# The last feed-forward block's second projection and last norm: from channels on the partitions to tokens on the partitions

## The reference

```python
def layer_norm_2(x, g, b):
    xf = x.astype(F32)
    mu = jnp.mean(xf, -1, keepdims=True)
    var = jnp.mean(jnp.square(xf - mu), -1, keepdims=True)
    return ((xf - mu) * lax.rsqrt(var + LN_EPS) * g.astype(F32) + b.astype(F32)).astype(x.dtype)

def swiglu(x, w13, w2):
    g, u = jnp.split(x @ w13, 2, axis=-1)
    return (jax.nn.silu(g) * u) @ w2

def second_block(x, ...):
    h = x
    for i in range(DEPTH_2):          # DEPTH_2 = 2
        ...                           # the mixer of the layer
        h = layer_norm_2(DEEPNORM_ALPHA * h + mix, ln1_g[i], ln1_b[i])
        h = layer_norm_2(DEEPNORM_ALPHA * h + swiglu(h, f_w13[i], f_w2[i]), ln2_g[i], ln2_b[i])
    return h
```

## Time and profile before

| | |
|---|---|
| median of 3 runs | 1181.61 us (1177.98 to 1183.34) |
| the profiled execution | 1179.46 us, of which 1177.7 us are the span of the core |
| PE busy | 1121.2 us (95%), 8872 matmuls |
| DVE busy | 811.3 us (69%) |
| ACT busy | 620.0 us (53%) |
| granted PE clock, mean | 0.986 of full speed |
| DMA | 194.7 MB, mean 165 GB/s; weight loads 359 of 512 KB |

### The profile page before, as it was taken

One profiled execution on the slowest core, in us unless ns is written; L12 is line 12 of the kernel. 1 busy time (PEld: TensorE's weight loads), 2 busy tenths in 40 slices (PEclk: granted clock), 3 DMA queues, 4 the chain that ended last, 5 costly groups with the idle time before them and its releaser, 6 DMA issues.

```text
span 1177.7 us, 21218 instructions
## 1 busy us (share of the span) xinstructions
PE 1121.2 (95%) x8872; PEld 1090.4 (93%) x8872; DVE 811.3 (69%) x1363; ACT 620.0 (53%) x1035; POOL 3.3 (0%) x13
## 2 busy tenths in 40 slices
PE   7999989999999998889989999999999999999998
PEld 7998878899999997679989999999999899999997
DVE  7987489878877786586766755555688657555554
ACT  5567444556465558733444645454455546454542
POOL 0000000000000000000000000000000000000000
PEclk9999999999999998989989999999999999999999
DMA  9984247256766613233223365556345335556500
GB/s 371 410 335 167 73 143 286 90 196 222 246 209 203 207 63 108 62 104 122 91 72 126 114 207 184 194 183 195 108 162 193 116 104 161 192 185 190 186 1 36
DMA packets 58128, 194.71 MB, mean 165 GB/s; under 512 B 10801, under 2 KB 11185, under 8 KB 57905
## 3 DMA queue, kind: packets, MB, share of 16 engines
q1 hardware_dynamic: 58032, 193.35, 48.8%
HBM read 192.02 MB, written 1.31 MB: 164 GB/s over the span
## 4 chain that ended last, share of the span: by engine, by line
PE 72%; DVE 17%; ACT 7%; issue 2%; DMA 1%; SPq 1%; ACTq 0%; DVEq 0%
PE ps L500 60%; DVE lo L1434 4%; PE ps L679 3%; ACT hi L970 2%; PE ps L507 2%; DVE raw L1421 2%; PE ps L598 2%; DVE B L1443 1%; PE ps L519 1%; DVE st L1451 1%; DVE ev L1672 1%; DVE B L1456 1%; DVE ev L1669 1%; DVE B L1747 1%; PE ps L685 1%
## 5 line engine op out<-in xcount | busy, mean ns | idle before, releaser
L500 PE MATMUL ps<-hh,hi 128*128 128x256 f32 x1792 | 510.5, 285 | 14.9 <-DVE hl L1468 3.5
L500 PE MATMUL ps<-hl,hi 128*128 128x256 f32 x1792 | 503.6, 281 | 0.0
L500 PE MATMUL ps<-hh,lo 128*128 128x256 f32 x1792 | 503.4, 281 | 0.0
L1434 DVE TENSOR_TENSOR lo<-raw,hi 128x1024 fp32r<-128x1024 f32 x311 | 378.2, 1223 | 172.4 <-ACT hi L970 171.6
L500 PEld LDWEIGHTS ps<-hh,hi 128*128 128x128 f32 x1792 | 340.7, 190 | 18.9 <-issue 9.3
L970 ACT ACTIVATE hi<-raw 128x1024 fp32r<-128x1024 f32 x311 | 324.6, 1052 | 54.7 <-PE ps L500 52.2
L500 PEld LDWEIGHTS ps<-hl,hi 128*128 128x128 f32 x1792 | 340.8, 190 | 0.3
L500 PEld LDWEIGHTS ps<-hh,lo 128*128 128x128 f32 x1792 | 340.6, 190 | 0.0
L500 PE MATMUL ps<-fh,hi 128*128 128x256 f32 x568 | 160.1, 282 | 3.3 <-ACT B L1074 2.5
L500 PE MATMUL ps<-fl,hi 128*128 128x256 f32 x568 | 159.0, 280 | 0.0
L500 PE MATMUL ps<-fh,lo 128*128 128x256 f32 x568 | 158.9, 280 | 0.0
(11 more groups left out here) (242 smaller groups left out, 1084.2 us busy)
## 6 DMA issues: line engine op xcount, KB each, us to landing
raw<-in_w SPq DMA_DIRECT2D x359, 512.0 KB, 4.1
B<-in_t SPq DMA_DIRECT2D x2, 512.0 KB, 5.6
xa<-in_x SPq DMA_DIRECT2D x1, 1024.0 KB, 12.8
out<-h SPq DMA_DIRECT2D x2, 512.0 KB, 2.9
cst<-in_c SPq DMA_DIRECT2D x1, 984.0 KB, 11.0
B<-between SPq DMA_DIRECT2D x32, 4.0 KB, 1.6
vec<-in_v SPq DMA_DIRECT2D x1, 328.5 KB, 8.9
between<-crow SPq DMA_DIRECT2D x16, 8.0 KB, 1.8
```

The source lines that it names most:

```text
L500: m = g.matmul(o, l, r, start=first and n == 0, stop=last and n == 2, skip_group_check=True)
L1434: g.tensor_tensor(lo[:, j % SPLIT, :], raw[:, PLACE[j] % RAW, :], hi[:, j % SPLIT, :].bitcast(F), ALU.subtract).then_inc(*up("lo", j))
```

## The change

The second projection of the last feed-forward network and the norm after it are moved to the token layout.

- PE: `down` for this network calls `rows_out_of`: activations `fh`, `fl` stationary, weights moving, 12 matmuls of 512 columns for a unit in place of 24 of 256. After `first_tiles`, 16 fp32 matmuls (`carry_in`) put the residual, `xa` times a diagonal matrix of the square root of 2, into banks 0 to 3 first. Units 19, 20 and 21 of `w21` come after the last tile of the first projection, first all three for tokens 0 to 127 (mark `tok`), then all three for tokens 128 to 255. The residual, the two sums over partitions, the spinning matmuls in the norm and the 16 transposes at the end are gone.
- DVE and ACT: for each half of the tokens bn_stats twice, bn_aggr, a 128 x 1 root, reciprocal and product, and then the 1024 channels in two halves: DVE does two scalar_tensor_tensor on the first, ACT one activation and DVE two tensor_tensor on the second.
- Gain and bias come as rows copied to all partitions (`in_r`, 1 MB), loaded into `B[2]` behind the weight unit (`w131`, 8).
- SP: four output DMAs of 256 KB, each 128 rows of 2 KB, in place of two of 512 KB.
- Constants: `mstrict` gives way to `alpha`, and `sel` (240 columns) is dropped.

```diff
@@ sync
                 g.dma_start(raw[:, i % RAW, :], wts[i]).then_inc(raws[i % RAW], 16)
+                if PLAN[i] == ("w131", 8):
+                    s.wait_ge(*at("scores", 7))
+                    g.dma_start(B[2][:, :, :].rearrange("p a b -> p (a b)"), rows).then_inc(s_rows_in, 16)
...
             for c in range(2):
-                s.wait_ge(*at("outv", c))
-                s.wait_ge(*at("outa", c))
-                g.dma_start(out[c], ofin[:, c, :]).then_inc(s_out, 16)
-            s.wait_ge(s_out, 32)
+                for n in range(2):
+                    s.wait_ge(*at("out_tok", (c, n)))
+                    v = slice(512 * n, 512 * n + 512)
+                    g.dma_start(out[c, :, v], ofin[:, c, v]).then_inc(s_out, 16)
+            s.wait_ge(s_out, 64)
@@ tensor
+            def carry_in(y, k):
+                s.wait_ge(*(at("n_v", (y, k))))
+                for c in range(2):
+                    g.matmul(bank[2 * c + k // 4][:, (k % 4) * P:(k % 4) * P + P], xa[:, k, c * P:c * P + P], C("alpha"),
+                             start=k % 4 == 0, stop=False, skip_group_check=True)
+            def rows_out_of(kind, k, xh, xl, made, cs, last):
+                j = UNIT[kind, k]
+                wh, wl = slot(j)
+                s.wait_ge(*at("lo", j))
+                s.wait_ge(*made)
+                for c in cs:
+                    v = slice(c * P, c * P + P)
+                    for n in range(2):
+                        m = three(bank[2 * c + n][:, :], wh[:, n * 512:n * 512 + 512], wl[:, n * 512:n * 512 + 512],
+                                  xh[:, v], xl[:, v], False, last, flip=True)
+                    if last:
+                        m.then_inc(*(up("unit", j) if c else up("tok", kind)))
+                if 1 in cs and not last:
+                    m.then_inc(*up("unit", j))
-            def ffn(kup, kdown, h_of, free0):
+            def ffn(kup, kdown, h_of, free0, tokens=False):
...
+                if tokens:
+                    for k in range(8):
+                        carry_in(h_of, k)
                 def down(j):
+                    if tokens:
+                        rows_out_of(kdown, j, fh[:, j % 4, :], fl[:, j % 4, :], at("f_lo", (kup, j)), (0, 1), False)
+                        return
...
-                    if j >= 2:
+                    if j >= 2 and not (tokens and j == FF - 1):
                         down(j - 2)
-                down(FF - 2)
-                down(FF - 1)
+                if tokens:
+                    for c in range(2):
+                        for j in (FF - 3, FF - 2, FF - 1):
+                            rows_out_of(kdown, j, fh[:, j % 4, :], fl[:, j % 4, :], at("f_lo", (kup, j)), (c,), j == FF - 1)
+                else:
+                    down(FF - 2)
+                    down(FF - 1)
-            ffn("w131", "w21", "x5", at("hl", ("x5", 0)))
-            after("x6", lambda k: at("res", ("x6", k - k % 2)))
...
+            ffn("w131", "w21", "x5", at("hl", ("x5", 0)), tokens=True)
@@ scalar
             ffn("w131", "w21", False)
-            after("x6", "ln2_g_2", "ln2_b_2", 1, False)
+            table(ACT.Sqrt)
             for c in range(2):
-                s.wait_ge(*at("out_mm", (c, 1)))
-                g.activation(ofin[:, c, 512:1024], bank[2 * c + 1][:, :], ACT.Copy).then_inc(*up("outa", c))
+                s.wait_ge(*at("fmv", c))
+                g.activation(frs[:, c, :], fmv[:, c, 1:2], ACT.Sqrt, bias=eps[:, 0:1]).then_inc(*up("fsd", c))
+                s.wait_ge(*at("fnm", c))
+                g.activation(ofin[:, c, 512:1024], bank[2 * c + 1][:, :], ACT.Identity, scale=frs[:, c, :],
+                             bias=fnm[:, c, :]).then_inc(*up("fa", c))
@@ vector
             ffn("w131", "w21", False)
-            after("x6", ("w21", FF - 1), "ln2_g_2", "ln2_b_2", 1, False)
+            s.wait_ge(s_rows_in, 16)
             for c in range(2):
-                s.wait_ge(*at("out_mm", (c, 0)))
-                g.tensor_copy(ofin[:, c, 0:512], bank[2 * c][:, :]).then_inc(*up("outv", c))
+                s.wait_ge(*(at("unit", UNIT["w21", FF - 1]) if c else at("tok", "w21")))
+                for n in range(2):
+                    g.bn_stats(fst[:, c, 6 * n:6 * n + 6], bank[2 * c + n][:, :]).then_inc(*up("fbn", (c, n)))
+                s.wait_ge(*at("fbn", (c, 1)))
+                g.bn_aggr(fmv[:, c, :], fst[:, c, :].rearrange("p (i n) -> p i n", i=2)).then_inc(*up("fmv", c))
+                s.wait_ge(*at("fmv", c))
+                v = ofin[:, c, 0:512]
+                g.scalar_tensor_tensor(out=v, in0=bank[2 * c][:, :], scalar=fmv[:, c, 0:1], in1=row_gb[:, 0, 0:512],
+                                       op0=ALU.subtract, op1=ALU.mult).then_inc(*up("fcent", c))
+                s.wait_ge(*at("fsd", c))
+                g.reciprocal(frs[:, c, :], frs[:, c, :]).then_inc(*up("frs", c))
+                s.wait_ge(*at("frs", c))
+                g.scalar_tensor_tensor(out=fnm[:, c, :], in0=fmv[:, c, 0:1], scalar=-1.0, in1=frs[:, c, :], op0=ALU.mult,
+                                       op1=ALU.mult).then_inc(*up("fnm", c))
+                g.scalar_tensor_tensor(out=v, in0=v, scalar=frs[:, c, :], in1=row_gb[:, 1, 0:512], op0=ALU.mult,
+                                       op1=ALU.add).then_inc(*up("out_tok", (c, 0)))
+                v = ofin[:, c, 512:1024]
+                s.wait_ge(*at("fa", c))
+                g.tensor_tensor(v, v, row_gb[:, 0, 512:1024], ALU.mult).then_inc(*up("fgain", c))
+                s.wait_ge(*at("fgain", c))
+                g.tensor_tensor(v, v, row_gb[:, 1, 512:1024], ALU.add).then_inc(*up("out_tok", (c, 1)))
```

More of the change, by code:

```diff
@@ L37 @@
 NVEC = _n
-CST = [("tri", 128), ("mstrict", 128), ("caus0", 128), ("caus", 128), ("lev", 3 * 128),
-       ("eye16", 256), ("cos", 256), ("sin", 256), ("icnt", 64), ("sel", 240)]
+CST = [("tri", 128), ("alpha", 128), ("caus0", 128), ("caus", 128), ("lev", 3 * 128),
+       ("eye16", 256), ("cos", 256), ("sin", 256), ("icnt", 64)]
 COFF = {}
@@ L229 @@
           "rule_dve": ("kss", "krn", "ktm", "low", "inv", "T", "TT", "P", "vn", "r1", "qss", "qdec", "attn", "oss", "orms", "ocf",
-                       "gated", "gl"), "merge": ("gated_a", "merged", "merged_lo")}
+                       "gated", "gl"), "merge": ("gated_a", "merged", "merged_lo"),
+          "last_norm": ("fbn", "fmv", "fcent", "frs", "fnm", "fgain", "out_tok"), "last_act": ("fsd", "fa")}
 SEM_OF = {e: name for name, events in SHARED.items() for e in events}
@@ L288, with program @@
     tensor_reduce = reciprocal = stream_shuffle = tensor_tensor_reduce = memset = dma_start = bn_stats = bn_aggr = matmul
-def program(nc, wts, head, vecs, csts, xtok, xT, low_dram, inv_dram, out):
+def program(nc, wts, head, vecs, csts, rows, xtok, xT, low_dram, inv_dram, out):
     with ExitStack() as ctx:
@@ L337, in program @@
         s_vec, s_cst, s_x, s_out, s_first = sem("s_vec"), sem("s_cst"), sem("s_x"), sem("s_out"), sem("s_first")
+        s_rows_in = sem("s_rows_in")
         s_xtok = [sem(f"s_xtok{c}") for c in range(2)]
@@ L421, in program @@
         ofin = h[:, :, :].rearrange("p a b -> p (a b)").rearrange("p (c n) -> p c n", c=2)
+        row_gb = B[2][:, :, :].rearrange("p a b -> p (a b)").rearrange("p (r n) -> p r n", r=2)
+        fst, fmv, frs, fnm = (sm[:, a:b].rearrange("p (c n) -> p c n", c=2) for a, b in ((0, 24), (24, 28), (28, 30), (30, 32)))
         mg, xs, ga, yb = B[1], B[2], B[4], B[5]
@@ L2046, in _constants @@
     tri = (i[:, None] <= i[None, :]).astype(np.float32)
-    mstrict = (i[None, :] < i[:, None]).astype(np.float32)
     caus = np.where(i[None, :] <= i[:, None], 0.0, NEG).astype(np.float32)
@@ L2061, in _constants @@
     cnt = np.concatenate([1.0 / np.minimum(np.arange(16) + 1, w) for w in (2, 4, 8, 16)]).astype(np.float32)
-    parts = {"tri": tri, "mstrict": mstrict, "caus0": np.zeros_like(caus), "caus": caus,
+    parts = {"tri": tri, "alpha": np.eye(P, dtype=np.float32) * np.float32(ALPHA2), "caus0": np.zeros_like(caus), "caus": caus,
              "lev": np.concatenate(lev, axis=1), "eye16": np.broadcast_to(np.eye(16, dtype=np.float32).reshape(1, 256), (P, 256)), "cos": cos, "sin": sin,
-             "icnt": np.broadcast_to(cnt, (P, 64)),
-             "sel": np.broadcast_to(((np.arange(240) >= 112) & (np.arange(240) < 128)).astype(np.float32), (P, 240))}
+             "icnt": np.broadcast_to(cnt, (P, 64))}
     return np.ascontiguousarray(np.concatenate([parts[n] for n, _ in CST], axis=1))
@@ L2088, in _vectors, with _rows @@
     return np.ascontiguousarray(np.concatenate([parts[n] for n, _ in VEC], axis=1))
+def _rows(x):
+    r = np.concatenate([np.asarray(x[n])[1] for n in ("ln2_g_2", "ln2_b_2")])
+    return np.ascontiguousarray(np.broadcast_to(r, (P, 2 * D)))
 def _nmaj(w):
@@ L2127 @@
                                                      _cols(np.asarray(inputs["c"])[0])], axis=1)),
+        "in_r": _rows(inputs),
```

(2 more changed lines are left out.)

## The result

The changed kernel takes 1188.73 us (median of 6 runs, 1187.03 to 1192.21) against 1180.47 us before (6 runs, 1177.92 to 1184.3): the ratio is 1.007, 95% interval 1.0044 to 1.0096. It is slower by some 8 us, where the prediction had it 9 us faster. The profiled execution is one of 1187.43 us.

What follows compares the result with a forecast made beforehand. PE, busy 95%, bounds the kernel up to its last projection matmul, then a 20.6 us tail. Tail to 7.9 us, less 3.56 us more PE, gives -9.2 us: 1170.3 to 1172.4, put at 1171.5 us; range 1167.5 to 1176.5.

Steps and rivals of the forecast that it cites:

- the rows' load: 1 MB more on SP's queue in the last network: 0 us; only a load over 25 us late would hold PE.
- Constants 123 KB smaller: Loading fewer constants: 0 us, below nothing by at most 0.3, as PE showed no wait on them.
- three signs: Prediction wrong if PE idles between last tile and last matmul, clock falls under 1.00 there, or a half takes 6 us.
- Flipped units: Second projection of the last network: 2.80 us a unit before and after, so 0 us for 22 units, +-0.4 us.
- The residual on PE: 32 fp32 instructions of `carry_in` in the last network add 3.56 us to PE; bounds 3.5 and 6.9.
- The norm of a half: Last norm, DVE's chain for half the tokens: 4.81 us, bounds 4.5 to 5.2; two halves in a row set the end.
- The output: Four output DMAs at the end: 2.5 us behind the norm in place of 3.56, bounds 2.2 and 3.6.
- The tail as a whole: From PE's last projection matmul to the end of the span: from 20.6 to 7.9 us.
- A: Residual matmuls cost as wide fp32 form: PE's end 3.4 us later, gain 5.8 us, 1173.7 to 1175.8 us; chance 0.06.
- B: DVE's last norm 1.0 us dearer a half, output at upper bound: gain 6.1 us, 1173.4 to 1175.5 us; chance 0.07.
- D: Half 0's head start worth nothing, both norms behind PE's end: span end 1172.7 us, gain 5.0 us; chance 0.05.
- C: Flipped units of the last network at clock 0.74: 21.6 us longer, kernel 12.4 us slower, 1193 us; chance 0.04.

Runs made afterwards that it cites:

- e1: Changed kernel with an unused 960-byte tensor behind `cst`, restoring the old addresses: 1172.41 us, ratio 0.9927 to the kernel before.
- e2: Kernel before with only the unused constant `sel` dropped: 1197.4 us, ratio 1.0137.
- e6: Changed kernel with a gap of 192 bytes behind `cst`, weights-to-activations distance 32 modulo 256 as before: 1171.24 us, ratio 0.9923.
- e15: Changed kernel with a gap of 192 bytes behind `cst` and the output in two DMAs of 512 KB: 1170.23 us, one execution.
- e10: Changed kernel with a gap of 160 bytes behind `cst`, distance 0 modulo 256: 1193.64 us, one execution.
- e12: Changed kernel with a gap of 96 bytes behind `cst`, distance 192 modulo 256, timed: 1160.5 us, ratio 0.9844 to the kernel before.
- e11: Kernel before with a gap of 96 bytes in place of `sel`, distance 192 modulo 256: 1165.29 us, ratio 0.9869.
- e5: Changed kernel with 32 bytes ahead of `raw`, so weights and activations all move up together: 1189.17 us, one execution.
- e7: Changed kernel with a gap of 96 bytes behind `cst`, distance 192 modulo 256: 1154.85 us, one execution.
- e8: Changed kernel with a gap of 64 bytes behind `cst`, distance 160 modulo 256: 1180.27 us, one execution.

## Why the prediction was wrong

**The step that failed** is the last sentence of the part on the rows' load: "Constants 123 KB smaller: 0 us, below nothing by at most 0.3". It priced the dropped constant as a transfer. It is also a move of every tensor declared behind it, by 960 bytes, and by the spacing that costs nearly all of the 13.9 us ahead of the last network and of the 3.2 us more than priced inside it (its 1056 matmuls of 256 columns at 3.3 ns are 3.5). Shown by e1 and e2, from both sides: 8.3 us faster with the old addresses, 17 us slower with nothing but the move. Behind it stands a step that the sum made without naming it: that 1177.7 us less the touched part stays as it is. With the old addresses the kernel has 1172.41 us (e1), and with the old distance at other addresses 1171.24 us (e6), where 1171.5 had been forecast. None of the three signs that the prediction named for being wrong (PE idle behind the last tile, a clock under 1.00 in this stage, 6 us for a half) came: all three look at the rewritten part.

**What held**, each with its size, from the kernel after or from e6:

- Flipped units: twice the columns at twice the spacing at the old distance (e6: 233.2 ns a matmul). The fixed 2.5 ns per matmul of the Trainium skill (TensorE: Matmul & The Clock Gate, "Wait — 56ns, not 53.3ns?") did not show: the stretch of PE from the first to the last projection matmul of the network is 188.65 us in e6 and 185.08 before, longer by 3.57 us. By that rule it would be 2.9, an estimate from that page.
- The residual on PE: 3.56 priced, and it is all of those 3.57. The row of the kernel after, with `cst` and `xa`:
```profile
994.62 3.73 PE L658 MATMUL ps<-cst,xa 128*128 128x128 f32 x32
```
- The norm of a half: 4.81 priced; the second starts 4.78 us after the first (1173.58, 1178.36), and from there to the end of its last operation are 4.85. The activation with two per-partition operands over 512 columns took 0.78 (0.81 priced), the scalar_tensor_tensor 0.75 (0.74), and bn_stats from PSUM what it took from SBUF in the earlier trace rows. DVE's one gap in a half is 0.19 and 0.18 us, before the first tensor_tensor. The prediction says that the scalar_tensor_tensor of 512 columns has no row; the trace before had one of a near form, with the same price:
```profile
L1905 DVE SCALAR_TENSOR_TENSOR hl<-ps,vec,hh 128x512 fp32r<-128x512 f32 x2 | 1.5, 750 | 1.7 <-ACT hh L1320 1.7
```
- The output: 2.5 us from DVE's end to the end of the span priced, 2.4 measured. The quarters land in 2.0 us each, and e15 shows the smaller pieces to be better here by 0.6 us.
- The tail as a whole: 7.9 us priced, 7.95 measured. The load of the rows landed 6.3 us after its issue, and ACT's split still waited for PE alone:
```profile
L1004 ACT ACTIVATE hi<-raw 128x1024 fp32r<-128x1024 f32 x62 | 65.2, 1052 | 11.6 <-PE ps L508 11.6
```

**The rivals.** A, B and D did not happen: the residual took 3.57 us and not 6.9, a half 4.8 us, and half 0 began 4.1 us ahead of PE's end. C was nearest: slower through PE's pace over a long stretch. But it named the granted clock, which is 1.00 in the windows of 40 us above and through the whole last network up to PE's last matmul, and it looked only at the touched part. The chance of 0.05 for slower was too small because all the cases were drawn from the operations of the diff; none was drawn from what the diff does to the layout.

**Open.** What in the chip ties the spacing to the distance was not found, nor whether the matmul or the weight load is what gets slower, nor whether the reads and writes of the other engines and the DMAs take part, which go to the moved tensors too and ran in every experiment. That 256 bytes is the period rests on e6 and on the pair of e10 and the idle matmuls. Why e1 had 117.8 ns in one stage and 116.7 elsewhere at the same addresses, why the stages differ at distance 192, and why e12's runs spread, is open too.

## What to carry to other kernels

A diff that changes the size of any on-chip tensor moves all that are declared behind it, so compare the spacing of matmuls in a stage that the diff does not touch before reading anything else. Where PE is the bound, sweep a dummy tensor through a few 32-byte steps: here that was worth 13 to 15 us to the old kernel (e11) and 28 us to the changed one (1188.73 to 1160.5 us, e12, timed in different sessions), against 8 to 10 us for the rewritten norm at the old distance (e1, e6), and no rule that I knew beforehand gave the good distance. When an edit is measured, hold the layout fixed (a dummy of the dropped size), or its gain and the layout's are mixed.

## What the runs showed of the hardware that I had not expected

- In streams of fp32r matmuls with 128 x 128 weights and 256 moving columns, at the full granted clock and without a wait, the mean spacing in the stage from 700 us on was between 113.3 and 120.0 ns, according to the distance of the two operands' start addresses in SBUF modulo 256 bytes (table above). Moving both together left the mean at 120.0 ns (e5). In other stages the same distance gave up to 4.1 ns more (e11).
- The Trainium skill (TensorE: Matmul & The Clock Gate, "Step-by-step: what each phase is for") says that loading the next weights does not steal read bandwidth from the running matmul, as the two have ports of their own. Here the pace of the running matmuls followed the address distance to the weight tensors, so the two are not independent of each other in this form; the runs don't show which part of the chip joins them, and no run weighs the read bandwidth itself.
- The same page of the Trainium skill (TensorE: Matmul & The Clock Gate, "Back-to-back issue gap") has 262 cycles for 256 columns at the full clock as the gap of isolated matmuls, an estimate of 109 ns. No mean spacing of these streams, in which each matmul has a weight load of its own, came down to that; the nearest is 113.3.
- The flipped form, with 512 columns of weights as the moving operand, follows the place too, but in another order: 228.9 ns at distance 0 (e10), 229.0 at 192 (e7), 233.2 at 32 (e6), 233.3 at 96 (the kernel after) and 234.7 at 160 (e8). Distance 0, the slowest for 256 columns, is the fastest here. Between 32 and 96 it makes no difference, and that is why the 22 flipped units lost nothing to the move while the tiles around them lost 3.5 us.
